# Shared weights for the last two latent tiles, four gathers inside the choice block, and a group norm inside it

## Chip, cores and metric

One core of a Trainium2 chip. The metric is the device time of one execution in microseconds, of which the median of several runs is given. Engines: PE (TensorE), DVE (VectorE), ACT (ScalarE), POOL (GpSimd), and SP, which only issues DMAs here. DMAs run on 16 DMA engines that all queues share.

## The reference

A two-layer backbone over 256 context tokens (two tiles of 128) and 512 latent tokens (four tiles), width 1024, all in float32. Each layer is a modulated norm, a mixer, and a product-key mixture of experts:

```python
def peer(h, wq, sub_keys, u_tab, v_tab):
    q = (h @ wq).reshape(T, P_HEADS, 2, P_DKEY // 2)            # 8 heads, two halves of 128
    s = jnp.einsum("thpd,hpnd->thpn", q, sub_keys)              # 16 x 128 key scores per token
    sv, si = lax.top_k(s, P_TOPK)                               # best 16 of each half
    cand = sv[:, :, 0, :, None] + sv[:, :, 1, None, :]          # 256 sums per head
    fv, fi = lax.top_k(cand, P_TOPK)                            # best 16: expert numbers
    gate = jax.nn.softmax(fv, axis=-1)
    a = gelu(u_tab[eidx] . h) * gate                            # 128 experts per token
    return sum(a * v_tab[eidx])
```

The mixer of layer 0 is a differential attention (4 heads, whose output gets a norm per head, `a_gn`, times 0.8) beside a windowed attention with sinks (8 heads); the two are joined and multiplied by `e_w_out`, gated and added to the stream. Layer 1 has a latent attention and a gated linear attention. Layer 1 needs only the latent tiles at the end.

## The kernel before

Everything for one token tile lies in 128 partitions. Raw blocks of five engine programs follow one another, each block ending in a barrier of all engines; within a block each engine works its own instruction list in order and waits on semaphores.

**Experts** (`run_experts`, L2652). For each tile there are 128 slots, one for each of a token's experts. In a slot POOL gathers 128 rows of 8 KB (u and v of one expert for each token, 1.05 MB) into one of 8 buffers `ring` (L2747), DVE multiplies the u half by the normed stream and sums it up (L2840), ACT makes gelu, weight and a diagonal matrix (L2859, L2861, L2865), and PE adds diagonal times v half to the tile's sum (L2876). POOL may gather slot s when PE is done with slot s - 8. Layer 0 has 6 tiles, 768 slots; layer 1 has 4, 512 slots. Before the first slot of tile t POOL waits for its expert numbers (`chosen`).

**Work beside the slots.** An order written out by hand puts other work at slots. In layer 0 (`BesideFirst`): the choice of the next tile's experts on DVE (`choose`, planned by `ChoicePlan`: for each quarter of the scores a load 2 slots after it is ready, first step at least 6 slots later, 8 slots a quarter; then 18 steps spread up to slot 119 of the tile); the attention of the four latent tiles (`HeadUnits`, 8 units a tile, begun at slots 9k for the first tile and 73 + 15k for the others); and for each latent tile (`LatentMixer`, L2063: POST 79, PITCH 120) group norm, output projection from `e_w_out_tiles` (8 loads of 512 KB), norm, and `LateScores` (L1910): 16 query and key products from `p_wqk` (16 loads of 576 KB), begun at slot 123 + 120x, one head every 4.4 slots. The four tiles load all of this separately. From slot 440 on `NextFront` projects the first half of layer 1. In layer 1 `LatentPair` does attention, projection and late scores of the last two tiles at once, a head every 4.0 slots from slot 145.

**Ahead of the experts** (`first_choice`, L1701): for two tiles projection with `w_o` (8 loads), gate, norm, transposes, 2 x 16 queries and scores with `w_q` in 4 buffers, and DVE's choice for the first tile, ending with the expert numbers (L1691) and the gates (L1697). Its last queries and scores are those of the second tile. Ahead of that in layer 0 stands a block of its own, `head_norm` ("gn0", L435), which does the group norm of the two context tiles: load the gains, ACT squares (L503), DVE sums (L521), ACT root (L508), DVE scales (L528, L531).

Of the kernel before, what the change touches and what calls it, by code (L numbers as in the profile page):

```python
# [14 lines left out]
P = 128  # L15
# [167 lines left out]
def start(nc, m, a):  # L183
# [3 lines left out]
    with Stage(nc, "mod") as s:  # L187
# [7 lines left out]
        with nc.Block() as block:  # L195
# [7 lines left out]
            def _(act):  # L203
# [4 lines left out]
                act.dma_start(m.sink[:, :], rows(a["b_sink"])).then_inc(v_loaded, 16)  # L208
                act.dma_start(m.band[:, :, :], a["band"].rearrange("s p k -> p s k")).then_inc(streams_loaded, 16)
                act.dma_start(m.R[:, 0:CT, :], a["ctx"].rearrange("b (t p) d -> p (b t) d", p=P)).then_inc(streams_loaded, 16)  # L210
                act.dma_start(m.R[:, CT:NT, :], a["x"].rearrange("b (t p) d -> p (b t) d", p=P)).then_inc(streams_loaded, 16)
                act.dma_start(m.ident[:, :], a["ident"]).then_inc(streams_loaded, 16)
                act.wait_ge(dots_ready, 1)
                act.activation(dots[:, :], dots[:, :], ACT.Exp).then_inc(lam_exp_done, 1)
                act.wait_ge(streams_loaded, 64)
# [8 lines left out]
            def _(dve):  # L224
# [10 lines left out]
                dve.wait_ge(v_loaded, 80)  # L235
# [3 lines left out]
                dve.tensor_scalar(m.neg_sink[:, :], m.sink[:, :], -1.0, None, ALU.mult)  # L239
                dve.drain()  # L240
# [192 lines left out]


def head_norm(nc, m, a, name, buf, tiles, segs, rope=None, factor=1.0, beside=None):  # L435

    turns = len(tiles) // 2  # L440
    extra = None
    S = sum(g * d for _, g, d, _ in segs)
    G = sum(g for _, g, _, _ in segs)
    with Stage(nc, name) as s:
        sq = s.sb("sq", [P, 2, S])
        ss = s.sb("ss", [P, 2, G])
        gains = s.sb("gains", [P, sum(d for _, _, d, _ in segs)])
        loaded = s.sem("loaded")
        squared, summed, rooted = s.sems("squared", 2), s.sems("summed", 2), s.sems("rooted", 2)
        if rope:  # L450
            r0, nr, tables = rope
            cos, sin = s.sb("cos", [P, NT, nr]), s.sb("sin", [P, NT, nr])
            near, far = s.sb("near", [P, 2, G, nr]), s.sb("far", [P, 2, G, nr])
            scaled, near_ready = s.sems("scaled", 2), s.sems("near_ready", 2)

        if beside:
            extra = beside(nc, m, a, s)

        def parts(i, q):

            at = g0 = gain0 = 0
            for c, g, d, _ in segs:
                yield (buf[:, i * 2 + q + (tiles[0] if tiles[0] and buf.shape[1] == NT else 0), c:c + g * d]
                       .rearrange("p (g d) -> p g d", d=d),
                       sq[:, q, at:at + g * d].rearrange("p (g d) -> p g d", d=d), ss[:, q, g0:g0 + g],
                       gains[:, gain0:gain0 + d], g, d, g0)
                at, g0, gain0 = at + g * d, g0 + g, gain0 + d

        def table(tab, i, q, g):
            return tab[:, ds(i * 2 + q + tiles[0], 1), :].broadcast_to([P, g, nr])  # L470

        def pairs(x, which):
            return x.rearrange("p g (f two) -> p g f two", two=2)[:, :, :, which]

        with nc.Block() as block:
            @block.sync
            def _(sp):
                at = 0
                for _, _, d, gain in segs:
                    sp.dma_start(gains[:, at:at + d], rows(gain)).then_inc(loaded, 16)  # L480
                    at += d
                if rope:
                    sp.dma_start(cos[:, :, :], a[tables + "_cos"].rearrange("(t p) d -> p t d", p=P)).then_inc(loaded, 16)
                    sp.dma_start(sin[:, :, :], a[tables + "_sin"].rearrange("(t p) d -> p t d", p=P)).then_inc(loaded, 16)

                if extra:
                    extra.sync(sp)

            if extra:
                @block.tensor  # L490
                def _(pe):
# [2536 lines left out]
```

## Time and profile before

| | |
|---|---|
| median of 3 runs | 4478.88 us (4476.03 to 4489.6) |
| profiled execution | 4486.69 us |
| its span, first to last instruction | 4485.4 us |
| PE busy | 3780.7 us, 84% |
| DVE busy | 2606.0 us, 58% |
| moved by DMA | 1577.55 MB, mean 352 GB/s |
| of it by gathers | 1342.36 MB |
| mean granted TensorE clock | 0.956 |

All rows that follow are of the one profiled execution, times counted from its first instruction. The experts of layer 0 take about 525 to 2660 us, those of layer 1 from 3109 us to the end. A view by windows gives, for each stretch, what each engine was busy and, at the end, the granted clock, the mean busy share of the 16 DMA engines (slightly over 1 when they are full) and the rate. In the timeline SPq and POOLq stand for a queue's issue of DMAs. The records of L2840 come in pairs, a product and the read of its sum.

### The profile page before, as it was taken

Reading aid. Unit: us, or ns where it says so; the run is one execution under the profiler, and the core shown is the slowest. Engines: PE = TensorE matmul, PEld = TensorE weight load, DVE = VectorE, ACT = ScalarE, POOL = GpSimd, SP = SyncE. Lnnn points to the kernel's source line nnn. Section 1 sums busy time; section 2 is a strip of 40 time slices with the busy share of each in tenths; the row PEclk is TensorE's granted clock in tenths of the full one; section 3 lists DMA queues with packets and bytes.
Section 4 is the critical chain, followed back from the end, with each engine's and each line's share of the span. In section 5 each row is a group of like instructions: output and inputs, shape, how many; then the busy total and the mean of one; then the engine's idle time right before and its main releaser. Section 6 shows DMA issues by size and latency. Waiting matters only on the chain. (4 is left out here: it accounts for less than half of the span.)

```text
span 4485.4 us, 45108 instructions
## 1 busy us (share of the span) xinstructions
PE 3780.7 (84%) x12934; PEld 1931.3 (43%) x12934; DVE 2606.0 (58%) x5668; ACT 1746.1 (39%) x5153; POOL 1703.8 (38%) x1350
## 2 busy tenths in 40 slices
PE   5987789898899898888889968687889997877777
PEld 2443644454454454444444433456444452322222
DVE  3524687666766856755654442346765558666544
ACT  1112255445444544433333331422664433333333
POOL 0100144444344433444444431001434434656675
PEclk9988999999999999999999988799999999999999
DMA  4254799999999999999999981027999999999998
GB/s 171 113 221 168 266 421 403 420 420 420 401 420 418 417 420 413 420 417 421 417 420 422 419 338 62 4 78 249 399 374 404 422 421 411 416 421 421 421 421 358
DMA packets 252894, 1577.55 MB, mean 352 GB/s; under 512 B 31715, under 2 KB 45955, under 8 KB 81510
## 3 DMA queue, kind: packets, MB, share of 16 engines
q0 software_dynamic: 185088, 1342.36, 72.5%
q1 hardware_dynamic: 65622, 228.83, 13.7%
q10 hardware_dynamic: 1936, 3.48, 0.2%
q8 instruction: 103, 1.69, 0.2%
q14 instruction: 145, 1.19, 0.1%
HBM read 1566.20 MB, written 8.36 MB: 351 GB/s over the span
## 5 line engine op out<-in xcount | busy, mean ns | idle before, releaser
L2876 PE MATMUL ps<-ex_ring,ex_diag 128*128 128x512 f32 x5120 | 2496.4, 621 | 481.4 <-ACT ex_diag L2865 450.5
L2747 POOL DMA_INDIRECT ex_ring<-in_p_uv,expert x1280 | 1648.6, 1288 | 2239.7 <-PE ps L2876 1523.9
L2840 DVE SCALAR_TENSOR_TENSOR ex_ring<-ex_ring,H 128x1024 f32<-128x1024 f32 x1280 | 1560.2, 1224 | 1198.3 <-DMA ex_ring<-in_p_uv,expert 1151.3
L2876 PEld LDWEIGHTS ps<-ex_ring,ex_diag 128*128 128x128 f32 x5120 | 926.3, 195 | 1705.4 <-ACT ex_diag L2865 879.6
L2859 ACT ACTIVATE ex_act_w<-ex_dots 128x1 f32<-128x1 f32 x1280 | 258.2, 202 | 1558.6 <-DVE ex_ring L2840 1552.4
L2865 ACT ACTIVATE ex_diag<-ident_sb,ex_weight 128x128 f32<-128x128 f32 x1280 | 513.9, 401 | 92.6 <-issue 3.6
L2861 ACT ACTIVATE ex_weight<-ex_act_w,gates 128x1 f32<-128x1 f32 x1280 | 377.0, 295 | 91.6 <-issue 4.5
L655 PE MATMUL ps<-win_w,hT 128*128 128x512 f32 (+1 forms) x480 | 191.9, 557 | 1.9 <-PEq L280 1.4
L2027 PEld LDWEIGHTS ps<-bs_hT,bs_w 128*128 128x128 f32 x1024 | 128.2, 197 | 34.6 <-issue 34.6
L655 PEld LDWEIGHTS ps<-win_w,hT 128*128 128x128 f32 x480 | 90.4, 191 | 106.0 <-issue 103.9
L2027 PE MATMUL ps<-bs_hT,bs_w 128*128 128x128 f32 x1024 | 127.7, 279 | 0.3 <-issue 0.3
L2840 DVE DVE_READ_ACCUMULATOR ex_ring<-ex_ring,H 128x1 f32 x1280 | 104.9, 82 | 0.0
L2859 ACT ACT_TABLE_LOAD x72 | 92.4, 1283 | 1.8 <-PEq L1737 0.5
L670 ACT ACTIVATE ph_sq<-ps 128x512 f32<-128x512 f32 (+1 forms) x24 | 12.4, 517 | 160.6 <-PE ps L655 160.6
L871 PEld LDWEIGHTS ps<-KV,bs_probsT 128*128 128x128 f32 x480 | 62.9, 192 | 24.0 <-issue 24.0
L1794 PE MATMUL ps<-hTc,fc_w_q 128*128 128x128 f32 x512 | 64.1, 279 | 9.6 <-DMA fc_w_q<-in_p_wqk 8.2
L1794 PE MATMUL ps<-hT,fc_w_q 128*128 128x128 f32 x512 | 64.4, 279 | 7.3 <-DMA fc_w_q<-in_p_wqk 5.9
L700 DVE TENSOR_REDUCE ph_ss<-ph_sq 128x8 f32<-128x512 f32 (+1 forms) x24 | 14.1, 586 | 97.0 <-ACT ph_sq L670 97.0
L2152 PEld LDWEIGHTS ps<-bs_w,bs_hT 128*128 128x128 f32 x512 | 62.3, 192 | 15.7 <-issue 15.7
L2027 PE MATMUL ps<-K,bs_w 128*128 128x256 f32 x256 | 65.7, 379 | 0.0
L1794 PEld LDWEIGHTS ps<-hTc,fc_w_q 128*128 128x128 f32 x512 | 59.6, 192 | 13.0 <-DMA fc_w_q<-in_p_wqk 11.5
L1794 PEld LDWEIGHTS ps<-hT,fc_w_q 128*128 128x128 f32 x512 | 59.5, 192 | 11.0 <-DMA fc_w_q<-in_p_wqk 9.3
(439 smaller groups left out, 3291.7 us busy)
## 6 DMA issues: line engine op xcount, KB each, us to landing
bs_w<-in_p_wqk SPq DMA_DIRECT2D x80, 576.0 KB
fc_w_q<-in_p_wqk SPq DMA_DIRECT2D x64, 576.0 KB, 4.9
ca_mod_w<-in_w_mod SPq DMA_DIRECT2D x24, 1024.0 KB, 6.8
ex_ring<-in_p_uv,expert POOLq DMA_INDIRECT x1280
win_mod_w<-in_w_mod SPq DMA_DIRECT2D x16, 1024.0 KB, 4.8
bs_w<-in_e_w_out_tiles SPq DMA_DIRECT2D x32, 512.0 KB
win_w<-in_e_w_in SPq DMA_DIRECT2D x9, 1024.0 KB, 11.2
mod_mod_w<-in_w_mod SPq DMA_DIRECT2D x8, 1024.0 KB, 15.0
```

Of the source, the lines that this page charges most:

```text
L655: mm = pe.matmul(m.ps[:, u % 4, 0:halves * 256], m.hT[:, k, t * P:(t + 1) * P], pre.w[:, n % 2, 0:halves, k, :], start=(k == 0), stop=(k = ...
L700: dve.tensor_reduce(ss[:, u % 2, 0:groups(u)], heads(sq[:, u % 2], u), AX.X, ALU.add).then_inc(summed, 1)
L871: mm = pe.matmul(self.O[:, cols], self.probsT[:, r % 2, x * P:(x + 1) * P], KV[:, self.blocks(n)[j], vals], start=(j == 0), stop=(j == las ...
L1794: mm = pe.matmul(m.ps[:, 4 + u % 2, 0:P], w_q[:, u % RING, k * P:(k + 1) * P], m.hT[:, k, cols(u // NH)], start=(k == 0), stop=(k == KC - 1))
L2027: mm = pe.matmul(m.ps[:, self.q_banks[u % nq], 0:cols], w[:, j * P:(j + 1) * P], self.turned_of(self.tiles_of(u), j), start=(j == 0), stop ...
L2152: mm = pe.matmul(m.ps[:, 7, c % 4 * P:(c % 4 + 1) * P], self.hT[:, k, :], w[:, k * P:(k + 1) * P], start=(k == 0), stop=(k == KC - 1), ski ...
L2747: pool.indirect_dma_start(ring[:, r, :], None, uv_rows, bass.IndirectOffsetOnAxis(ap=expert[:, t % 2, n:n + 1], axis=0),).then_inc(landed[ ...
L2840: dve.scalar_tensor_tensor(out=ring[:, r, 0:D], in0=ring[:, r, 0:D], scalar=1.0, in1=h_of(t + t0), op0=ALU.mult, op1=ALU.mult, accum_out=d ...
L2859: act.activation(act_w[:, b:b + 1], dots[:, t % 2, n:n + 1], ACT.Gelu)
L2861: act.activation(weight[:, b:b + 1], act_w[:, b:b + 1], ACT.Copy, scale=gates[:, t % 2, n:n + 1])
L2865: act.activation(diag[:, b, :], m.ident[:, :], ACT.Copy, scale=weight[:, b:b + 1]).then_inc(diag_ready, 1)
L2876: mm = pe.matmul(mix_banks(t)[:, half, :], diag[:, b, :], ring[:, r, D + half * BANK:D + (half + 1) * BANK], start=(n == 0), stop=(n == SL ...
```

## The change

- `LatentMixer` works on groups of tiles, here [0], [1] and [2, 3], instead of on four single tiles. The last two share the output projection and the late scores: each weight is loaded once and used for both. `POST` and `PITCH` are replaced by explicit slots 79, 202, 337; the shared late scores begin at slot 400 and end at 470. The attention units begin at 73 + 10k, not 73 + 15k, so that both tiles are done by slot 337. Scores go to two buffers in turn (`score_of`).
- `first_choice` gets a POOL program: when the projection is done and the numbers are written, it gathers slots 0 to 3. `run_experts` starts at slot 4. The ring is allocated around both, and `w_o` and `w_q` of `first_choice` lie in it (w_o in buffers 0 to 3).
- The block gn0 goes. Its work stands at the head of the ACT and DVE programs of `first_choice` in layer 0, with the gains loaded and scaled in the very first block. The gate product of the first tile goes ahead of the scale's. `iota` is loaded once, in the first block.
- Smaller: `rest` holds 4 heads instead of 16, `hot` lies in the scores, and `sc_read` is raised after the numbers.

Its core:

```diff
+EARLY = 4
+def gather(pool, m, a, slot, t):
+    r = slot % m.ring.shape[1]
+    pool.indirect_dma_start(m.ring[:, r, :], None, a["p_uv"],
+                            bass.IndirectOffsetOnAxis(ap=m.expert[:, t % 2, slot % SLOTS:slot % SLOTS + 1], axis=0),
+                            ).then_inc(m.landed[r], 16)
...
-        w_o, w_q = s.sb("w_o", [P, KC, D]), s.sb("w_q", [P, RING, (KC + 1) * P])
+        w_o = m.ring[:, 0:EARLY, :].rearrange("p r d -> p (r d)").rearrange("p (k d) -> p k d", d=D)
+        w_q = m.ring[:, EARLY:, :].rearrange("p r d -> p (r d)")[:, 0:RING * (KC + 1) * P].rearrange("p (r d) -> p r d", r=RING)
...
+            @block.gpsimd
+            def _(pool):
+                pool.wait_ge(out_done, 4)
+                pool.wait_ge(chosen, 1)
+                for slot in range(EARLY):
+                    gather(pool, m, a, slot, 0)
...
                 def turn(n):
+                    if grouped:
+                        pe.wait_ge(o_ready, n + 1)
...
+                if grouped:
+                    for n in range(2):
+                        act.activation(gsq[:, n, :], src_of(tiles[n])[:, 0:A_HEADS * A_DV], ACT.Square).then_inc(gn_squared, 1)
...
+                dve.wait_ge(gate_loaded, 16)
+                gated(0, 0, D, 2)
                 dve.wait_ge(vec_loaded, 16 * (4 if stream else 3))
...
-        begin = [9 * k for k in range(2 * A_HEADS)] + [73 + 15 * k for k in range((XT - 1) * 2 * A_HEADS)]
...
+            at, ahead = b + 4 + 6 * n, 4 // n
+            out_slots.append([at + (2 * ahead + 3) * (c // ahead) + 2 * (c % ahead) for c in range(KC)])
...
+            at = out_slots[-1][-1] + 4
...
+            late_begin.append(at + self.LOAD + 3 + 6 * n)
...
+        n = 2 * A_HEADS
+        begin = [9 * k for k in range(n)] + [73 + 10 * k for k in range(3 * n)]
+        self.mixer = LatentMixer(m, a, s, place, [[0], [1], [2, 3]], begin, [79, 202, 337], [4.4, 4.4, 4.4])
...
-                for slot in range(T * SLOTS):
-                    t, n, r = slot // SLOTS, slot % SLOTS, slot % RING
-                    if n == 0 and t:
+                for slot in range(EARLY, T * SLOTS):
+                    t, n = slot // SLOTS, slot % SLOTS
+                    if n == 0:
                         pool.wait_ge(chosen, t)
...
-                head_norm(nc, m, a, "gn0", m.Qc, CTILES, [(0, A_HEADS, A_DV, a["a_gn"])], factor=1.0 - LAM_INIT)
```

## Rows read from the trace of the kernel before

**Rows 1.** Page, section 2: GB/s in 40 slices of 112.1 us.

```profile
GB/s 171 113 221 168 266 421 403 420 420 420 401 420 418 417 420 413 420 417 421 417 420 422 419 338 62 4 78 249 399 374 404 422 421 411 416 421 421 421 421 358
```

**Rows 2.** Products at L2840, what ended DVE's idle time before them: us, times.

```profile
  DMA ex_ring<-in_p_uv,expert: 1151.3, 893
```

**Rows 3.** Windows: us, busy (x) PE, PEld, DVE, ACT, POOL, PEclk, DMA share, GB/s.

```profile
560.00:700.00 140.00, 123.95 (x378) 61.27 (x377) 115.66 (x315) 78.26 (x216) 61.80 (x54) 0.94 1.01 421
1200.00:1240.00 40.00, 34.91 (x129) 20.14 (x128) 23.39 (x43) 18.79 (x57) 13.63 (x13) 0.91 0.91 369
3240.00:3400.00 160.00, 144.26 (x478) 70.53 (x479) 108.92 (x232) 96.60 (x243) 63.66 (x57) 0.99 0.98 374
3560.00:3700.00 140.00, 133.72 (x431) 75.35 (x431) 70.33 (x171) 49.34 (x168) 50.03 (x48) 1.00 1.02 422
3780.00:3820.00 40.00, 28.62 (x58) 10.95 (x59) 36.82 (x58) 16.65 (x49) 18.21 (x14) 0.96 0.99 379
```

**Rows 4.** DMA issues of the whole run: count, KB each.

```profile
bs_w<-in_p_wqk SPq DMA_DIRECT2D x80, 576.0 KB
bs_w<-in_e_w_out_tiles SPq DMA_DIRECT2D x32, 512.0 KB
```

**Rows 5.** Timeline: start us, us, engine line op, [idle before], group norm to projection.

```profile
402.55 1.28 ACT L508 ACT_TABLE_LOAD   x1
403.02 0.33 SPq L480 DMA_DIRECT2D gn_gains<-in_a_gn  x1
407.59 0.69 DVE L528 TENSOR_TENSOR Qc<-Qc,gn_ss 128x512 f32<-128x512 f32 x1
410.97 3.65 PE L1762 MATMUL ps<-ident_sb,Qc 128*128 128x128 f32 x16 [16.37 <-PEq L475]
411.32 3.74 SPq L1741 DMA_DIRECT2D fc_w_o<-in_e_w_out  x8
414.81 28.23 PE L1775 MATMUL ps<-fc_w_o,hTc 128*128 128x512 f32 x64 [0.19 <-DMA fc_w_o<-in_e_w_out]
```

**Rows 6.** Timeline, handover to the experts of layer 0.

```profile
500.17 14.58 SPq L1735 DMA_DIRECT2D fc_w_q<-in_p_wqk  x7
515.85 0.23 DVE L1691 TENSOR_SCALAR expert<-fc_num 128x128 uint32<-128x128 f32 x1
525.33 1.02 POOL L2747 DMA_INDIRECT ex_ring<-in_p_uv,expert  x1 [126.52 <-issue]
```

**Rows 7.** Windows of both handovers, columns as in rows 3.

```profile
516.00:536.00 20.00, 7.10 (x51) 5.84 (x49) 0.79 (x5) 3.01 (x8) 7.61 (x8) 0.81 0.50 174
524.00:528.00 4.00, 1.57 (x8) 1.07 (x8) 0.00 (x0) 1.50 (x2) 2.06 (x3) 1.00 0.26 49
3101.00:3116.00 15.00, 7.02 (x55) 6.08 (x53) 0.67 (x3) 3.01 (x8) 5.07 (x6) 0.88 0.39 127
```

**Rows 8.** Timeline, handover to the experts of layer 1.

```profile
3100.75 0.23 DVE L1691 TENSOR_SCALAR expert<-fc_num 128x128 uint32<-128x128 f32 x1
3109.41 0.97 POOL L2747 DMA_INDIRECT ex_ring<-in_p_uv,expert  x1 [295.16 <-POOLq L1737]
```

**Rows 9.** Timeline of PE, layer 1: score products, four slots apart.

```profile
3560.24 0.61 PE L2014 MATMUL ps<-bs_w,bs_qT 128*128 128x128 f32 x4
3571.34 0.61 PE L2014 MATMUL ps<-bs_w,bs_qT 128*128 128x128 f32 x4
```

**Rows 10.** Timeline of DVE, layer 1: first and last step of a squeezed choice.

```profile
3754.89 2.28 DVE L2764 TENSOR_TENSOR R<-val 128x2048 f32<-128x2048 f32 x1
3809.43 0.29 DVE L2811 TENSOR_TENSOR gates<-ex_shift,ex_total 128x128 f32<-128x128 f32 x1
```

**Rows 11.** Lines of DVE in 560:720, 880:1080, 3240:3400: busy, mean ns, idle before.

```profile
L2840 DVE SCALAR_TENSOR_TENSOR ex_ring<-ex_ring,H 128x1024 f32<-128x1024 f32 x64 | 77.2, 1221 | 22.7 <-DMA ex_ring<-in_p_uv,expert 21.7
L2840 DVE SCALAR_TENSOR_TENSOR ex_ring<-ex_ring,H 128x1024 f32<-128x1024 f32 x70 | 85.3, 1223 | 70.9 <-DMA ex_ring<-in_p_uv,expert 70.4
L2560 DVE COPY bs_oT<-ps 64x128 f32<-64x128 f32 x10 | 2.9, 289 | 41.4 <-PE ps L2498 41.4
```

## What the change will do to the time

> **What bounds the kernel now.** I read the slices of the page first [rows 1]. From slice 5 to slice 22 (560 to 2640 us, the experts of layer 0) and again from slice 28 on (the experts of layer 1) the rate stands at 374 to 422 GB/s; PE is nearly as full (124 of the 140 us from 560) [rows 3], so both have to be held against every step. The engine that consumes the gathers says which of them binds: DVE's product at L2840 sat idle 1151 us for gathers to land [rows 2], and the 140 us from 560 ran at 421 GB/s and DMA share 1.01. So in these two stages the time is the bytes that move, divided by 421 GB/s, wherever the 8 buffers of the ring keep the queue full. Three kinds of stretch are exceptions. Dips inside the experts: 369 GB/s in the 40 us from 1200, 379 in the 40 us from 3780, 374 over 160 us from 3240 [rows 3]. Two handovers, where nothing is gathered although the experts are already numbered [rows 6, 7]. And the serial stages in front, where one group norm stands alone in a block [rows 5]. A slot, one gather of 1.05 MB, is 2.49 us of DMA.
>
> **Part 1, shared weights.** The latent group for tiles 4 and 5 loads once what two groups loaded: 8 output tiles of 512 KB, 16 query and key tiles of 576 KB [rows 4], and, once less, a gate row and a norm row spread over 128 x 1024 f32, 0.52 MB each by that shape. That is 4.19 + 9.44 + 1.05 = 14.68 MB, all of it in the bound stage. By 421 GB/s: **-34.9 us**. PE does the same columns as before, only bunched: per head 8 products of 256 columns and two scores. The same pairing exists in layer 1, one head every 4 slots. There PE's score records at 3560.24 and 3571.34 are 11.1 us apart for 4 slots, 2.78 us a slot [rows 9], and DMA held 422 GB/s at 1.02 for 140 us [rows 3]. In layer 0 a pair of heads comes every 4.4 slots, so PE has more room than there: no loss taken. For the shared output (8 pieces of two tiles in 24 slots, from slot 353) PE's load is about 1.7 + 8 x 3.6 / 24 = 2.9 us a slot and DMA's (1.05 + 8 x 0.52 / 24) / 0.421 = 2.9 us: a tie, for which I take **+1 us** (0 to 4).
>
> **Part 2, the choice of tile 4 is squeezed.** Its last quarter of scores is now ready at slot 470 instead of 433, since the pair starts at 400. By the plan (load 2 later, first step 6 later, 8 slots for a quarter) the other 18 steps of the choice get slots 486 to 502 instead of 449 to 502. Layer 1 shows this squeeze: there the scores of tile 4 come late too (slot 212), the 18 steps lie in slots 228 to 245, from the candidate sums at 3754.89 to the gates at 3809.43 + 0.29 = 3809.72, 54.8 us for 17 products and the choice, while DMA supplies 17 slots in 17 x 2.49 = 42.3 us [rows 10]. DVE falls 12.5 us behind; the ring absorbs most; the 40 us from 3780 ran at 379 instead of 422, that is 40 x 43 / 422 = 4.1 us lost [rows 3]. In layer 0 it is 16 slots: 34 us of choice + 16 x 1.23 = 53.6 us against 39.8, 1.3 us more behind, which the ring can't absorb any more: **+5.5 us** (3 to 14; no gain is possible, since the steps are the same ones).
>
> **Part 3, denser heads.** Units of attention of slots 73 to 313 come every 10 slots, not every 15, 8 of them in 80 slots. The first eight units already run at a pitch of 9: in 160 us from 560 DVE waited 21.7 us for DMA at that product and the rate was 421 [rows 3, 11]. With the late scores beside them there is room too: in the 200 us from 880 it waited 70.4 us for DMA [rows 11], and 2.3 more units at about 4.3 us of DVE take 10 of that. Only where the choice of tile 2, the norm and the heads meet (slots 240 to 255) is DVE full already, and 40 x (421 - 369) / 421 = 4.9 us are lost today [rows 3]. A third more heads there adds 0.13 us a slot over some 15 slots: **+2 us** (0 to 8).
>
> **Part 4, the group norm joins.** Today ACT squares and loads its table from 402.55, while DVE waits for the gains, which SP asks for at 403.02; the block ends, PE turns 16 pieces from 410.97 in 3.65 us and projects from 414.81, when the first of w_o has landed, asked for at 411.32 [rows 5]. After, SP asks for w_o where it asked for the gains (8.3 us earlier), and DVE reduces at once: root at 403.9 behind the table load (402.55 + 1.28), scale and gain of tile 0 to 406.1, of tile 1 to 407.8 (estimates from passes of 0.7 us over 512 columns, two a tile, and the small ones between), PE turns tile 1 from 408.0 to 409.9 and projects. **-4.9 us** (3 to 5.6): the wait for w_o becomes a wait for the norm. The rest of the stage follows, since out, h turn and 32 queries are one chain on PE and the rows of gate and scale come 8.3 us earlier with w_o; what is late next in it is DVE's choice, which starts from the fourth score. The new order of DVE (gate product ahead of the scale) is free: h of tile 0 is wanted only when PE has projected tile 1. The loads moved into the first block (iota, gain) are two small ones beside the streams there, in a block that waits for 8 MB of modulation weights: 0 (0 to +0.5).
>
> **Part 5, four gathers leave early.** In layer 0 the numbers are written at 515.85 + 0.23 = 516.1; the block ends with PE's last score and POOL issues in the next one, at 525.33 [rows 6]; its end is some 8 us behind the numbers. From 516 to 536 the DMA share is 0.50: 10.0 us of idle [rows 7]. After, POOL issues at 516.3; its first bytes come 1.6 us after issue, as today (share 0.26 in 524 to 528 is 1.0 us of work, from 527.0 [rows 7]). That leaves 1 us idle behind the last of w_q. The four cover 4 x 2.49 = 10 us. But the last w_q load, issued at 514.7 [rows 6], now shares the engines with gathers; it may take two to three times its 1.4 us, and PE's last scores and the block's end with it, so that gather 4 comes about 1 us after the four have run dry. 10.0 - 1 - 1: **-8.0 us** (4 to 9.4). Layer 1 the same: numbers at 3101.0, POOL at 3109.41 [rows 8], share 0.39 over the 15 us from 3101 [rows 7], 9.15 us idle, less 0.6 to the first bytes and 1 at the block's end: **-7.5 us** (4 to 8.7). POOL's queue holds nothing else in this block, so its new wait (for the projection that frees w_o's place, long done) delays nobody. DVE's later wait for iota and shift rows at the start goes too; it costs nothing today, as gathers lay in the queue all the while (PE's and DVE's late start at the first slots moves no byte).
>
> A rule of the Trainium skill bears on this. What the row shows is that the last w_q load is asked for 1.4 us before the numbers are ready, so the two meet [rows 6]. The page "DMA: Bandwidth & Descriptors", section "Queues, rings and completion order", says that each engine alternates between the queues that have work, packet by packet; by it no load is pushed back behind all four gathers, and the block's end slips by a transfer or two, not by 10 us. By strict order of arrival it would slip by nothing, and the part would give 1 us more. Which of the two holds no row of before shows.
>
> **The sum.** -34.9 + 1 + 5.5 + 2 - 4.9 - 8.0 - 7.5 = -46.8 us. The profiled execution took 4486.69 us: 4439.9. The median of the timed runs is 4478.88, 7.8 lower, and the same difference gives **4432 us**. Everything behind the experts of layer 0 (2700 to 3040) shifts as it stands, and so does the slow stretch from 3240, whose limit isn't bytes.
>
> **Rivals.** A, the ring can't absorb the crowding: DVE's lag of 14 us at tile 4, and the lags of tiles 2 and 4 in full, are passed on to DMA (nothing absorbed): 13.8 + 2 x 4.9 + 4 for the projection = 27 instead of 8.5, so 4451. Against it stand the 4.1 of 12.5 us in layer 1. B, the handovers give only half: the early gathers push back the last w_q loads and with them the block, and the next gather finds the engines dry for 4 us each time: 4440. C, the gain is larger, since the ring absorbs all of it and the dips of today go with the second group: -34.9 - 5.6 - 18 = -58.5, 4420. D, slower than before, by the stretch at 3240: there units every 5.5 slots bring the engines into lockstep, DVE waits 41.4 us of 160 for PE's value products [rows 11], and the rate is 374 instead of 421 [rows 3]. If a pitch of 10 with late weights beside it did the same for slots 73 to 313, 240 slots x 2.8 us x 0.125 = 84 us would be lost, against 46.8 + 2 of gain: 4514. It decides where a unit's chain no longer fits its pitch; at a pitch of 9 without weights DVE waits for none of it [rows 11], so the point lies below 9 unless the weights matter. E, the change doesn't do what it says: the pair runs PE-bound from 353 to 466 by 0.3 us a slot, 34 us, and takes back the weights: 4465.
>
> **How the numbers follow.** The forecast 0.58, A 0.13, B 0.10, C 0.11, D 0.04, E 0.04. With every term at its best the sum is -55.6 us (4423), with every term at its worst -19.9 us (4459). A, B and C lie within or 3 us outside, D and E are left out; C and the spread of the runs of before put the low end at 4415, the worst sum the high end at 4460. A measurement of this kernel can tell about 0.3% (13 us) from no change. Faster by more than that: all but D and E (E is 12.8 us faster, within it), less 0.02 for the spread of medians, 0.90; within it 0.05; slower 0.05.
>
> **What would show it.** Right: bs_w loads of 24 and 64 instead of 32 and 80; POOL's first gather within 1 us of the numbers in both layers, DMA share above 0.9 over the following 20 us; PE's first projection at 410; the experts of layer 0 some 26 us shorter from first gather's landing to last; a dip of 5 us near slot 495. Wrong: the rate below 415 over slots 73 to 313 (D), below 400 over 353 to 466 (E), or a DMA gap after the fourth gather (B).

## The result, and the profile after

The changed kernel took **4408.23 us** (median of 4 runs, 4406.40 to 4418.11) against 4480.22 us for the kernel before (median of 4, 4476.03 to 4489.60): ratio 0.9843, 95% interval 0.9824 to 0.9861. It is 72.0 us faster where 46.8 were predicted, and 4408 lies below the low end of 4415. The profiled executions took 4407.58 and 4486.69 us, their spans 4406.3 and 4485.4.

The page of the changed kernel, section 2 (40 slices of 110.2 us), its DMA issues, and its windows at the places of rows 3:

```profile
GB/s 174 108 212 198 288 424 401 412 419 424 404 425 426 426 420 426 427 391 427 427 427 427 427 295 37 4 86 297 394 372 412 425 423 405 427 427 427 427 427 363
...
bs_w<-in_p_wqk SPq DMA_DIRECT2D x64, 576.0 KB, 8.0
bs_w<-in_e_w_out_tiles SPq DMA_DIRECT2D x24, 512.0 KB, 8.0
```

```profile
560.00:700.00 140.00, 125.92 (x387) 62.66 (x385) 114.98 (x307) 80.38 (x223) 59.44 (x54) 0.93 1.01 420
3780.00:3820.00 40.00, 31.36 (x65) 10.79 (x65) 30.14 (x97) 14.39 (x48) 26.25 (x17) 1.00 1.01 428
```

The loads are 24 and 64 in place of 32 and 80 [rows 4], and the bytes fell from 1577.55 to 1562.74 MB. The surprise is in the slices. Before, no slice stood above 422 GB/s [rows 1]; after, half of the busy slices read 426 or 427, in the experts of layer 1 too, where the change has nothing to do with the weights. **The ceiling itself rose by 1.2%.** The prediction divided every byte by 421 GB/s and held that number for fixed.

The group norm, then the handover to the experts of layer 0 (timelines of the changed kernel, columns as in rows 5):

```profile
394.34 1.15 ACT L1747 ACTIVATE fc_gsq<-Qc 128x512 f32<-128x512 f32 x2 [8.14 <-PEq L867]
395.50 1.28 ACT L1750 ACT_TABLE_LOAD   x1
396.03 3.73 SPq L1634 DMA_DIRECT2D ring<-in_e_w_out  x8
398.90 3.42 PE L1663 MATMUL ps<-ident_sb,Qc 128*128 128x128 f32 x16 [11.31 <-DVE Qc L1797]
402.15 1.02 PE L1676 MATMUL ps<-ring,hTc 128*128 128x512 f32 x2
...
503.77 0.23 DVE L1570 TENSOR_SCALAR expert<-fc_num 128x128 uint32<-128x128 f32 x1
504.89 1.02 POOL L1586 DMA_INDIRECT ring<-in_p_uv,expert  x1 [113.09 <-DVE expert L1570]
507.90 1.01 PE L1705 MATMUL ps<-ring,fc_qT 128*128 128x128 f32 x4
508.72 0.94 POOL L1586 DMA_INDIRECT ring<-in_p_uv,expert  x1 [0.30 <-issue]
519.23 1.23 DVE L2787 SCALAR_TENSOR_TENSOR ring<-ring,H 128x1024 f32<-128x1024 f32 x1 [14.02 <-PEq L1630]
519.93 1.34 POOL L1586 DMA_INDIRECT ring<-in_p_uv,expert  x1 [10.28 <-POOLq L1630]
```

POOL issues its first gather 0.9 us behind the numbers, as meant. But gather 4 follows only at 519.93: from 509.7 to 519.2 no engine computes. Nothing but the four gathers is in flight, and the next block begins when they have landed: in the DMA records of the trace their last packet ends at 518.4, 0.8 us before DVE starts. The windows of that handover (columns as in rows 3) show the engines of the DMA full, then empty again:

```profile
504.00:508.00 4.00, 4.00 (x38) 4.00 (x37) 0.71 (x3) 0.98 (x4) 2.50 (x3) 1.00 0.44 114
508.00:512.00 4.00, 0.78 (x5) 0.40 (x3) 0.00 (x0) 0.75 (x3) 1.35 (x2) 0.89 0.98 395
512.00:516.00 4.00, 0.00 (x0) 0.00 (x0) 0.00 (x0) 0.00 (x0) 0.00 (x0) 0.50 1.01 422
516.00:520.00 4.00, 0.77 (x3) 0.74 (x5) 0.77 (x1) 0.81 (x1) 0.07 (x1) 0.50 0.36 152
520.00:524.00 4.00, 4.00 (x10) 1.87 (x8) 4.00 (x7) 3.17 (x10) 3.39 (x3) 0.50 0.51 143
```

**Where the time went.** I cut the profiled span of each kernel at two marks, the instruction that writes the expert numbers in layer 0 and the one in layer 1. The first mark moves by chance: the last value product of the context attention began at 393.50 before and 386.48 after, and anywhere from 386.48 to 408.05 in the 14 profiles of this study, among them profiles of kernels that don't differ before it. The latest of them had a granted clock of 0.56 from 350 to 386, where before had 0.94 and after 1.00. So the front is compared from that product on, and the rest from mark to mark.

| us | before | after | |
|---|---|---|---|
| start to the attention's last value product | 393.5 | 386.5 | -7.0, chance |
| from there to the numbers of layer 0 | 122.3 | 117.3 | -5.0 |
| numbers of layer 0 to those of layer 1 | 2584.9 | 2531.4 | -53.5 |
| numbers of layer 1 to the end | 1384.6 | 1371.1 | -13.5 |

The last row alone contradicts the prediction, which had 7.5 us there, all of it from early gathers.

### The profile page after: what moved, and what is told of

It is laid out like the page before. It is cut to its first block and busy times, and to the rows that moved or that the text cites. A ratio compares the mean times of both kernels' runs of the same rounds, so it can differ in the third digit from the quotient of the medians.

```text
span 4406.3 us, 44443 instructions
## 1 busy us (share of the span) xinstructions
PE 3757.3 (85%) x12678; PEld 1911.6 (43%) x12678; DVE 2603.1 (59%) x5667; ACT 1746.1 (40%) x5137; POOL 1689.1 (38%) x1350
## 2 busy tenths in 40 slices
DMA packets 248572, 1562.74 MB, mean 355 GB/s; under 512 B 30851, under 2 KB 44963, under 8 KB 77190
## 5 line engine op out<-in xcount | busy, mean ns | idle before, releaser
L2823 PE MATMUL ps<-ring,ex_diag 128*128 128x512 f32 x5120 | 2476.7, 618 | 416.6 <-ACT ex_diag L2812 389.7
L1586 POOL DMA_INDIRECT ring<-in_p_uv,expert x1280 | 1633.8, 1276 | 2179.3 <-PE ps L2823 1447.4
L2787 DVE SCALAR_TENSOR_TENSOR ring<-ring,H 128x1024 f32<-128x1024 f32 x1280 | 1557.5, 1225 | 1084.0 <-DMA ring<-in_p_uv,expert 1041.2
L2823 PEld LDWEIGHTS ps<-ring,ex_diag 128*128 128x128 f32 x5120 | 923.9, 194 | 1663.6 <-ACT ex_diag L2812 847.5
L1945 PEld LDWEIGHTS ps<-hTc,bs_w 128*128 128x128 f32 x768 | 110.8, 191 | 29.3 <-issue 23.5
L1945 PE MATMUL ps<-hTc,bs_w 128*128 128x128 f32 (+1 forms) x768 | 120.3, 310 | 0.3 <-issue 0.3
L2787 DVE DVE_READ_ACCUMULATOR ring<-ring,H 128x1 f32 x1280 | 105.2, 82 | 0.0
L1695 PE MATMUL ps<-hTc,ring 128*128 128x128 f32 x512 | 65.0, 282 | 8.0 <-DMA ring<-in_p_wqk 6.8
L1695 PE MATMUL ps<-hT,ring 128*128 128x128 f32 x512 | 63.9, 278 | 7.7 <-DMA ring<-in_p_wqk 6.2
L2090 PEld LDWEIGHTS ps<-bs_w,hTc 128*128 128x128 f32 x512 | 60.9, 192 | 11.5 <-issue 11.5
```

The costliest lines, as they stand in the source:

```text
L1586: pool.indirect_dma_start(m.ring[:, r, :], None, a["p_uv"], bass.IndirectOffsetOnAxis(ap=m.expert[:, t % 2, slot % SLOTS:slot % SLOTS + 1] ...
L1695: mm = pe.matmul(m.ps[:, 4 + u % 2, 0:P], w_q[:, u % RING, k * P:(k + 1) * P], m.hT[:, k, cols(u // NH)], start=(k == 0), stop=(k == KC - 1))
L1945: mm = pe.matmul(m.ps[:, self.q_banks[u % nq], 0:cols], w[:, j * P:(j + 1) * P], self.turned_of(self.tiles_of(u), j), start=(j == 0), stop ...
L2090: mm = pe.matmul(m.ps[:, 7, at:at + P], self.hT[:, k, i * P:(i + 1) * P], w[:, k * P:(k + 1) * P], start=(k == 0), stop=(k == KC - 1), ski ...
L2787: dve.scalar_tensor_tensor(out=ring[:, r, 0:D], in0=ring[:, r, 0:D], scalar=1.0, in1=h_of(t + t0), op0=ALU.mult, op1=ALU.mult, accum_out=d ...
L2823: mm = pe.matmul(mix_banks(t)[:, half, :], diag[:, b, :], ring[:, r, D + half * BANK:D + (half + 1) * BANK], start=(n == 0), stop=(n == SL ...
```

## The experiments

### Is the rate the ring's address?

The buffers of the ring are where the gathered rows land. Adding up the allocations, `ex0_ring` starts at byte 99264 of a partition in the kernel before and `ex1_ring` at 101312; both are 192 past a multiple of 256 (the residue, as it is called below). The change adds two lasting tiles, `iota` (64 bytes a partition) and `gain_gn` (512), and allocates the ring elsewhere: 108032 and 110080, both multiples of 256. Theory: that residue sets the rate. Rivals: the chip or the run; another part of the change.

```diff
# x1_before_pad64: the kernel before, and this line
+        m.pad = ctx.enter_context(nc.sbuf_tensor("pad", [P, 16], F32))
# x2_after_pad448 (112 floats), x5_after_pad256 (64), x6_after_pad64 (16): the changed kernel, in both layers
-                with nc.sbuf_tensor("ring1", [P, 8, 2 * D], F32) as m.ring:
+                with nc.sbuf_tensor("pad1", [P, 112], F32), nc.sbuf_tensor("ring1", [P, 8, 2 * D], F32) as m.ring:
```

> The kernel before with one unused tile of 64 bytes a partition among its lasting allocations, so that the ring of expert rows starts at byte 99328 of a partition (a multiple of 512) in place of 99264 (448 past one); in layer 1 at 101376 in place of 101312. Nothing else differs. Address theory (the start address of the ring sets how fast the rows land): the stretch 560:700 moves 427 GB/s in place of 421, and as the expert stages are mostly saturated the time falls by 30 to 50 us, to about 4440. Rival (the rate differed by chip or by run, or comes from another part of the change): 421 GB/s and 4480 within 5.

> The changed kernel with an unused tile of 448 bytes a partition just ahead of each layer's ring, so that both rings start 448 bytes past a multiple of 512, as in the kernel before. Address theory: 421 GB/s again in saturated stretches and 30 to 50 us more than the changed kernel, about 4448. Rival (rate by chip, run or another part of the change): 427 GB/s and 4408 within 5.

> The changed kernel with 256 unused bytes a partition ahead of each ring: rings start at a multiple of 256 that is no multiple of 512. Where the grain of the address is 256 bytes: 427 GB/s in saturated stretches, 4408 within 5. Where it is 512 bytes or more: 421 GB/s and 30 to 40 us more, about 4441.

> The changed kernel with 64 unused bytes ahead of each ring: rings start 64 bytes past a multiple of 512. Grain of 256 or 512 bytes: 421 GB/s and about 4441, as with 448. Grain of 64 bytes, with something else at work in the earlier two pads: 427 GB/s and 4408.

The GB/s of the page, section 2, of the four in this order:

```profile
GB/s 173 107 213 188 265 427 406 426 426 426 409 425 426 417 425 420 426 426 427 425 426 427 427 333 55 4 79 261 399 374 405 425 423 418 421 426 427 426 427 366
```

```profile
GB/s 173 114 219 184 291 419 402 403 419 421 409 421 421 416 419 422 422 390 421 422 422 422 422 292 40 4 94 296 394 368 414 420 421 402 422 421 421 421 421 356
```

```profile
GB/s 174 107 213 190 287 427 400 419 417 423 404 425 425 421 423 426 427 392 427 427 427 427 427 303 38 4 92 291 396 369 413 425 423 406 427 427 427 427 427 364
```

```profile
GB/s 173 114 217 184 290 419 403 411 416 420 406 416 420 412 415 420 421 386 421 421 422 422 421 295 43 4 93 295 393 370 406 421 420 402 421 421 421 421 421 356
```

| kernel | ring start mod 256 | highest GB/s | us, median | layer 0 to layer 1 | layer 1 to end |
|---|---|---|---|---|---|
| before | 192 | 422 | 4480.22 | 2584.9 | 1384.6 |
| x1_before_pad64 | 0 | 427 | 4434.86 | 2550.4 | 1371.5 |
| after | 0 | 427 | 4408.23 | 2531.4 | 1371.1 |
| x5_after_pad256 | 0 | 427 | 4407.63 | 2526.3 | 1373.1 |
| x2_after_pad448 | 192 | 422 | 4441.40 | 2550.0 | 1385.3 |
| x6_after_pad64 | 64 | 422 | 4448.24 | 2553.8 | 1387.3 |

Every expectation of the address theory was met. One unused tile of 64 bytes makes the old kernel 48.9 us faster than the runs of before beside it (4483.73; ratio 0.9887, 0.9860 to 0.9914); moving the new kernel's ring off the multiple costs it 33.2 and 40.0 us. The pad of 256 puts the ring at an odd multiple of 256 and costs nothing, so **a multiple of 256 is enough, it needn't be one of 512**, and 64 past is about as bad as 192 past. No ring was placed 128 past, so the grain may be 128 bytes as well as 256. The pads shift the tiles behind them as well. Of these `bs_w`, the other large target, can be left out as cause: in layer 0 it starts at residue 0 in x2, at 422, and at 128 in x1, at 427. DVE's product on the ring took the same in all six, a median of 1.22 us, so it isn't the engines' reading of the ring. Chip and run are out too, as x1 and x2 ran on one chip in one job.

The single packets say the same. A row of 8 KB is one packet, 163,840 of them in a run. With the ring at residue 0, 98% took 309 ns or less (all eleven profiles); in before, x2 and x6 it was 24 to 27%, and 71 to 74% took 311 to 320 ns. It isn't a matter of gathers alone: of the 6272 packets of 8 KB that plain loads moved between 40 and 400 us, 1183 took 311 to 320 ns in before, where their targets lie 192 past, and 41 to 90 in the thirteen others, where they lie at 0. On 128 past there is a hint only: the first block's 8 loads of modulation weights land 64 past in before and 128 past in the others, and of their 1024 packets 342 took 311 to 320 ns in before, 30 to 254 in the others.

The Trainium skill, page "DMA: Bandwidth & Descriptors", section "How a descriptor splits into AXI transactions", says that a descriptor is cut into transactions of 256 bytes, and that one which doesn't start 256-byte aligned needs one more. By it a row of 8 KB takes 33 in place of 32, 3.1% more (an estimate). The runs agree on the sign, and with its 256 bytes as far as they were tried; the measured difference is 1.2% (422 against 427 GB/s). The page speaks of what a transaction can read; that it is the landing address that counts here is what the pads show. Why the loss is a good third of what this count gives, and the same 64 and 192 past, no run shows.

### Do the early gathers buy anything?

The prediction's Part 5 said 15.5 us. The timeline above suggested another account, that the block's end waits until the gathers have landed.

```diff
# x3_early0: N = 0, and run_experts' POOL doesn't wait for `chosen` at slot 0.  x11_early2: N = 2
-                for slot in range(EARLY):
+                for slot in range(N):
                     gather(pool, m, a, slot, 0)
...
-                for slot in range(EARLY, T * SLOTS):
+                for slot in range(N, T * SLOTS):
```

> The changed kernel with no early gathers: the first choice issues none, the expert stage issues all from slot 0. Drain theory (the end of the block waits until the early gathers have landed, so they buy only the few us between the numbers and that end): 3 us more in each layer, 4414 in all (4408 to 4418). The prediction's own term (8.0 and 7.5 us gained): 15.5 us more, about 4424.

> The changed kernel with two early gathers in place of four. Drain theory (the block's end waits for the last early gather to land): the first gather of the expert stage is issued about 5 us sooner after the numbers (11 us in place of 16.2), and the time from layer 0's numbers to layer 1's stays within 1 us of the changed kernel's 2531.4 us; 4408. The prediction's term (2 us gained by each early gather, both layers): 4416.

From x3_early0's timeline, then from x11_early2's:

```profile
525.33 0.23 DVE L1570 TENSOR_SCALAR expert<-fc_num 128x128 uint32<-128x128 f32 x1
531.85 1.05 PE L1705 MATMUL ps<-ring,fc_qT 128*128 128x128 f32 x4
534.31 1.02 POOL L1586 DMA_INDIRECT ring<-in_p_uv,expert  x1 [120.94 <-issue]
539.86 1.23 DVE L2787 SCALAR_TENSOR_TENSOR ring<-ring,H 128x1024 f32<-128x1024 f32 x1 [13.12 <-DMA ring<-in_p_uv,expert]
```

```profile
508.37 0.23 DVE L1570 TENSOR_SCALAR expert<-fc_num 128x128 uint32<-128x128 f32 x1
510.81 0.97 POOL L1586 DMA_INDIRECT ring<-in_p_uv,expert  x1 [0.30 <-issue]
517.02 1.01 PE L1705 MATMUL ps<-ring,fc_qT 128*128 128x128 f32 x4
521.06 1.35 POOL L1586 DMA_INDIRECT ring<-in_p_uv,expert  x1 [9.28 <-POOLq L1630]
```

Without early gathers the next block's first gather goes out 1.4 us behind PE's last score product (532.90 to 534.31); with four it is 11.0 us (508.91 to 519.93). And the first product of the experts comes 14.5 us behind the numbers with none (539.86 - 525.33), 15.5 us with four (519.23 - 503.77): the early gathers delayed the very stage that they were to feed. From the numbers of layer 0 to the end of the span it is 3902.7 us with none, 3902.8 with two, 3902.5 with four. **They buy nothing that can be seen**; the same kernel with a pad of 256 differs by more (3899.4). The medians of whole runs (4418.43, 4410.58 and 4408.23) don't contradict it: those of x3_early0 lie between 4406.25 and 4441.22, with two at the level of the changed kernel and two late. Of these the profiled one (4429.27) is late by the chance in the front that the table above sets aside; the other has no profile.

The drain theory was right on the wait and missed on its price and its details. It gave each layer 3 us for the early gathers, and they bought none. With two of them the block restarted 12.7 us behind the numbers, not 11, and layer 0 to layer 1 took 2534.9 us, not within 1 us of 2531.4 (the rest of the run was 3.2 us shorter; no run shows why). The 12.7 us come from the gathers' own landing: the last load of w_q was asked for at 508.9, 0.6 us ahead of the first gather, the two shared the engines, and the second gather's last packet ended at 519.6. Layer 1 of the same run shows the wait with PE long done:

```profile
3048.08 1.01 PE L1705 MATMUL ps<-ring,fc_qT 128*128 128x128 f32 x4
3053.65 1.23 DVE L2787 SCALAR_TENSOR_TENSOR ring<-ring,H 128x1024 f32<-128x1024 f32 x1 [9.33 <-PEq L1630]
3054.34 1.35 POOL L1586 DMA_INDIRECT ring<-in_p_uv,expert  x1 [7.85 <-POOLq L1630]
```

In the four handovers with early gathers (layers 0 and 1 of the changed kernel, then of x11_early2) the last packet of the last gather ended at 518.4, 3050.0, 519.6 and 3053.0, and the next block's first product on DVE began at 519.2, 3050.8, 520.4 and 3053.7, 0.7 to 0.8 us behind each. So it is shown that the gathers in flight hold the block.

### Sharing, and denser heads

```diff
# x4_single and x7_single_dense: the latent tiles 2 and 3 apart again (and W = 2, so that nothing else changes size)
-        self.mixer = LatentMixer(m, a, s, place, [[0], [1], [2, 3]], begin, [79, 202, 337], [4.4, 4.4, 4.4])
+        self.mixer = LatentMixer(m, a, s, place, [[0], [1], [2], [3]], begin, [79, 199, 319, 439], [4.4, 4.4, 4.4, 4.4])
# x4_single also: heads 15 slots apart, as before
-        begin = [9 * k for k in range(n)] + [73 + 10 * k for k in range(3 * n)]
+        begin = [9 * k for k in range(n)] + [73 + 15 * k for k in range(3 * n)]
# x8_pace36: the changed kernel, late scores of the pair 3.6 slots apart
-[79, 202, 337], [4.4, 4.4, 4.4])
+[79, 202, 337], [4.4, 4.4, 3.6])
# x9_pitch12_pace36, on top of x8; then x9b_pitch15_9, on top of x8, with 346 for 337
+        begin = [9 * k for k in range(n)] + [73 + 12 * k for k in range(n)] + [169 + 10 * k for k in range(2 * n)]
+        begin = [9 * k for k in range(n)] + [73 + 15 * k for k in range(n)] + [193 + 9 * k for k in range(2 * n)]
```

> The changed kernel with the latent tiles 2 and 3 apart again (groups of one tile, begun every 120 slots) and the heads 15 slots apart as before; group norm, early gathers and the ring's address stay. The prediction's terms (34.4 us for 14.68 MB at 427 GB/s, less 5.5 for the squeezed choice, 2 for denser heads, 1 for the wide outputs): 26 us more than the changed kernel, about 4434. Rival (the ring absorbs the squeezed choice and the heads): 34 us more, 4442. Rival (dips cost twice the terms): 18 us more, 4426.

> The changed kernel with the latent tiles 2 and 3 apart (as x4_single), but with the heads 10 slots apart as in the change: the density of the heads by itself, against x4_single. The prediction's term: 2 us more than x4_single (0 to 8), about 4433. Reading of the rates in 60 us stretches of both traces (the changed kernel loses 11 us more than x4_single before slot 190, where only the heads' pitch differs): 11 us more than x4_single, about 4442. Ring absorbs it: 4431 and the same rates as x4_single.

> The changed kernel with the late scores of the shared group 3.6 slots apart in place of 4.4, so that the scores of tile 4 are there about 12 slots earlier and its choice has some 38 slots in place of some 26. The squeezed choice costs what the prediction says (5.5 us, rates of 383 and 406 GB/s between 1847 and 1967): 2 to 5 us less than the changed kernel, about 4404. Rival (the dip is that of the group's late scores themselves, denser still): same or up to 5 us more.

> x8_pace36 with the heads of latent tile 1 begun 12 slots apart (73 to 157) in place of 10, those of the shared pair 10 apart from slot 169. Theory (dense heads cost 11 to 16 us by dips before slot 190): tile 1's half of it comes back, 3 to 6 us less than x8_pace36, about 4397. Rival (only the number of heads before some slot counts, the loss moves with them into the pair's part): 4402, the dips later in the stage.

> x8_pace36 with the heads of tile 1 begun 15 slots apart as in the kernel before, those of the shared pair 9 apart from slot 193, and the pair's norm begun at slot 346 in place of 337. Theory of dense heads: tile 1's part like x4_single (a gain of 6 to 8 us before slot 190), the pair's part 1 slot denser (a loss of 2 to 4 us): 4398. Rival (9 apart is past what the engines keep up with): over 4405.

To see where bytes are lost I cut layer 0's experts into 31 windows of 60 us from 24 us behind the numbers on, and added up 60 us x (ceiling - rate) / ceiling (ceiling 427, for before 422):

| kernel | heads' pitch | windows 1-13 | 14-21 | 22-31 | layer 0 to layer 1 | us, median |
|---|---|---|---|---|---|---|
| before | 15 | 13.6 | 5.3 | 4.1 | 2584.9 | 4480.22 |
| x1_before_pad64 | 15 | 11.4 | 5.2 | 1.3 | 2550.4 | 4434.86 |
| x4_single | 15 | 9.1 | 6.9 | 3.0 | 2550.2 | 4430.75 |
| x7_single_dense | 10 | 26.1 | 3.7 | 4.2 | 2567.8 | 4446.80 |
| after | 10, shared | 20.2 | 2.8 | 9.4 | 2531.4 | 4408.23 |
| x8_pace36 | 10, shared | 21.4 | 3.5 | 3.7 | 2528.6 | 4401.65 |
| x9_pitch12_pace36 | 12/10, shared | 22.2 | 2.2 | 4.1 | 2526.7 | 4408.04 |
| x9b_pitch15_9 | 15/9, shared | 25.6 | 3.4 | 6.2 | 2532.1 | 4411.75 |

**Denser heads cost 16.1 us with the tiles apart** (x7 against x4: 4446.80 - 4430.75; 17.6 mark to mark), where the prediction had 2 and at most 8. **From x7 to the changed kernel 38.6 us are gained** (36.4 mark to mark), against the 34.4 us of the shared bytes at 427 GB/s. That step isn't sharing alone. The second group also begins at slot 202 in place of 199, and 5.9 us of the step lie in windows 1 to 13 (26.1 against 20.2), which end at slot 285, before anything is shared. The five other profiles with the changed kernel's order up to there (x3, x5, x8, x10, x11) lose 19.4 to 22.3 us in them, so it is no chance; that the three slots do it is likely, but no run moves them alone. From window 14 on x7 loses 7.9 us and the changed kernel 12.2, so that sharing with its squeezed choice is worth 34.4 - 4.3 = **about 30 us**, and denser heads cost **about 11** in the change as it is (20.2 - 9.1). Both together gain 22.5 us (x4 to after; 18.8 mark to mark), where the terms for x4_single gave 26.

Windows of x4_single, x7_single_dense and x9_pitch12_pace36, the sixth, the eleventh and the twelfth of the 31 (columns as in rows 3):

```profile
829.60:889.60 60.00, 54.59 (x193) 28.51 (x192) 38.23 (x62) 29.16 (x87) 29.23 (x23) 0.97 1.01 426
1129.60:1189.60 60.00, 48.45 (x154) 24.47 (x153) 54.32 (x89) 34.66 (x83) 26.14 (x20) 0.94 1.01 426
1189.60:1249.60 60.00, 57.33 (x239) 33.59 (x238) 31.81 (x52) 29.43 (x94) 25.55 (x23) 1.00 1.01 415
```

```profile
829.80:889.80 60.00, 51.68 (x193) 28.44 (x193) 37.99 (x68) 31.00 (x90) 21.83 (x20) 0.91 0.98 392
1129.80:1189.80 60.00, 53.06 (x215) 30.77 (x215) 51.68 (x102) 32.79 (x85) 22.76 (x20) 0.94 0.96 373
1189.80:1249.80 60.00, 54.76 (x209) 30.67 (x208) 42.81 (x75) 35.70 (x96) 25.35 (x22) 0.97 1.01 415
```

```profile
832.30:892.30 60.00, 57.38 (x216) 31.96 (x217) 37.82 (x63) 29.07 (x91) 23.58 (x22) 0.95 1.01 426
1132.30:1192.30 60.00, 53.81 (x222) 31.34 (x221) 53.35 (x97) 33.88 (x89) 26.26 (x20) 0.94 0.97 393
1192.30:1252.30 60.00, 52.80 (x201) 30.46 (x200) 31.18 (x58) 30.17 (x86) 20.55 (x20) 0.91 0.95 370
```

In the eleventh window DVE already works 54 of 60 us with heads 15 apart (a choice lies there), at 426 GB/s; with heads 10 apart PE rises from 48 to 53 of 60 beside it and the rate falls to 373. The changed kernel, also 10 apart, holds 416 there with both engines busier still (PE 56, DVE 55), so the busy shares alone don't account for the loss. Twelve apart clears the sixth window (426) and moves the loss into the eleventh and twelfth (393 and 370). My theory for x9 fell, its rival stood: the loss goes with the units to where they meet the choice. Nor did 15 and 9 do better. Neither is shown to beat x8_pace36: x9 is 1.9 us shorter from mark to mark, 6.4 us longer by the medians, and the two come from different jobs, whose runs of before differ by 4.7. Which of PE and DVE is late in those windows the runs don't settle.

The squeezed choice is the other dip. The first two rows are of the changed kernel, the last two of x8_pace36:

```profile
1847.80:1907.80 60.00, 42.02 (x79) 14.96 (x77) 56.83 (x132) 19.84 (x60) 26.46 (x20) 0.91 0.95 383
1907.80:1967.80 60.00, 50.31 (x114) 21.04 (x114) 42.95 (x96) 28.30 (x87) 31.84 (x26) 0.94 1.00 406
```

```profile
1850.90:1910.90 60.00, 48.26 (x111) 19.34 (x112) 56.19 (x112) 26.62 (x81) 30.74 (x26) 1.00 1.00 415
1910.90:1970.90 60.00, 47.38 (x102) 18.53 (x100) 38.63 (x87) 25.88 (x77) 34.84 (x25) 0.94 1.01 425
```

DVE is busy 56.8 of 60 us with the choice of tile 4 and PE only 42.0: here it is DVE that starves the ring. The two windows lose 9.1 us, and giving the choice some 12 more slots leaves 2.0 of it. x8_pace36 is the fastest kernel of the study: 4401.65 us (4399.15 to 4408.25), ratio to before 0.9807 (0.9779 to 0.9834), 6.0 us under x5_after_pad256 of the same job. Its interval overlaps that of the changed kernel (0.9824 to 0.9861), so that it is faster than the change is likely, not shown; the vanished dip is shown.

### The group norm

x10_gn_apart is the changed kernel with the block gn0 back.

```diff
                 context_attention(nc, m, a)
+                head_norm(nc, m, a, "gn0", m.Qc, CTILES, [(0, A_HEADS, A_DV, a["a_gn"])], factor=1.0 - LAM_INIT)
...
-                first_choice(nc, m, a, 0, CTILES, 1, a["e_w_out"], 0, lambda t: m.Qc[:, t, :], lambda t: m.H[:, t, :], True)
+                first_choice(nc, m, a, 0, CTILES, 1, a["e_w_out"], 0, lambda t: m.Qc[:, t, :], lambda t: m.H[:, t, :])
```

> The changed kernel with the group norm of layer 0 in a block of its own again, ahead of the first choice. The prediction's term: 4.9 us more (3 to 5.6), 4413. Reading of both traces from the first square to the projection (7.3 us against 13.4): 6.1 us more, 4414, and the projection starts 13.4 us after the first square.

```profile
400.57 1.15 ACT L506 ACTIVATE gn_sq<-Qc 128x512 f32<-128x512 f32 x2 [8.20 <-PEq L993]
402.21 0.33 SPq L483 DMA_DIRECT2D gn_gains<-in_a_gn  x1
405.05 0.23 DVE L518 TENSOR_SCALAR gn_gains<-gn_gains 128x128 f32<-128x128 f32 x1 [8.43 <-DMA gn_gains<-in_a_gn]
410.18 3.36 PE L1789 MATMUL ps<-ident_sb,Qc 128*128 128x128 f32 x16 [16.42 <-PEq L478]
414.24 6.08 PE L1802 MATMUL ps<-ring,hTc 128*128 128x512 f32 x13 [0.70 <-DMA ring<-in_e_w_out]
```

From the first square to the projection it is 13.7 us apart (400.57 to 414.24) and 7.8 us joined (394.34 to 402.15): 5.9 us. From the attention's last value product to the numbers, apart 122.3, 122.8 and 123.4 us (before, x1, x10), joined 114.3 to 117.3 in eleven profiles, mean 116: about **7 us**. The median of whole runs, 4421.07 (4413.59 to 4443.24), is 12.8 above the changed kernel's; it holds the chance of the front as well and is too wide to size a term of 5. By the ratios to the runs of before beside them (0.9858 and 0.9843) it is about 7, with intervals as wide as that.

## Why the prediction was right or wrong

**Direction right, size wrong, and the missing size has one cause.** The step that failed is "the time is the bytes that move, divided by 421 GB/s". That number was read rightly [rows 3] and taken for fixed, while it hung on where this kernel's ring lay: the changed kernel moved its bytes at 427. Like with like, the change from the kernel before to x2_after_pad448, which has the old residue, is -42.3 us (4483.73 to 4441.40), and to x6_after_pad64 -34.6 (4482.86 to 4448.24), against -46.8 predicted. The rest, 33 to 40 us, is the ring's address, which no term, rival or bound held: every term at its best gave 4423, rival C 4420, and all of them were worked out at 421 GB/s. The diff shows what moved it: the ring's new place and two lasting tiles ahead of it.

- **Part 1, -34.9 and +1.** Held: 24 and 64 loads, 14.81 MB less in all; the 14.68 MB reckoned are 34.4 us at 427 GB/s. The tie feared in the shared output didn't show; from 1308 to 1788 the eight windows of the changed kernel stand at 415 to 426 GB/s. E is refuted. The account closes: 34.4 us of bytes and 34.0 - 32.4 = 1.6 us less lost in the windows give 36.0, against 36.4 measured mark to mark from x7 to the changed kernel. Together with Part 2 it was -28.4, against some -30.
- **Part 2, +5.5 (3 to 14).** Held: windows 22 to 31 lose 9.4 us against 3.0 in x4_single and 3.7 in x8_pace36, so 5.7 to 6.4. The reading from layer 1 [rows 10] carried.
- **Part 3, +2 (0 to 8).** Mis-sized: 11.1 in windows 1 to 13 of the change itself (20.2 - 9.1), and 16.1 with the tiles apart. The step that failed is "with the late scores beside them there is room too". It joined two stretches [rows 11]: 560 to 720, where heads come 9 apart beside a choice but no projection, late score or norm runs, and 880 to 1080, where late scores run but heads come 15 apart. The prediction looked at the one place where all of them meet, slots 240 to 255, but x7 loses 60 x (426 - 373) / 427 = 7.4 us more than x4 in the one window from 1130, slots 219 to 238, just ahead of it, where that window holds a choice, a norm and 64 products of the output projection (7.8 us of PE) beside the heads. D had the mechanism at five to eight times its price.
- **Part 4, -4.9 (3 to 5.6).** The square-to-projection distance shrank by 5.9 us, the whole front by about 7. The wait for w_o became a wait for the norm, as meant: PE's turning waited 11.3 us for DVE, and the estimates of DVE's passes were a little slow.
- **Part 5, -15.5.** Wrong, the whole term: 0. The step that failed is "gather 4 comes about 1 us after the four have run dry". It treated the end of the block as PE's last score. In fact the block doesn't end with gathers in flight, so that the engines idle 9.5 us and DMA has a hole from about 517.4 to 522 in place of the one before the first gather (shares of 0.36 and 0.51 of two windows of 4 us, the busy part at the front of the first and at the end of the second). B named the hole and priced it at half; it took all. The share above 0.9 for 20 us, named as the sign, was there for 8 to 9 us. The meeting of the last w_q load with the gathers, for which the prediction took 1 us, didn't come about in layer 0: the load had landed at 505.4, the gathers' first packet started at 506.6, and PE's last score product ended 5.1 us behind the numbers, before 8.1. In x11_early2 they did meet, and the load's last packet ended 5.7 us behind its issue, against 6.1 before and 6.0 in x3_early0 with no gather beside it. The rule of the Trainium skill quoted in the prediction ("DMA: Bandwidth & Descriptors", "Queues, rings and completion order") has each engine alternate between its queues, packet by packet, so that no load is pushed back behind gathers, and the trace of x11_early2 agrees.
- **The sum.** With the ring at residue 0: denser heads +11, sharing with the squeezed choice in it -30, group norm -7, early gathers 0, together -26; measured from x1_before_pad64 to the changed kernel -26.6 (4434.86 to 4408.23). At the old residues the same edits gain 34.6 and 42.3, so 8 to 16 us more. A slower supply leaves the engines more slack and hides more of their crowding; with this it fits that the loss in the 31 windows grew by 14.5 us at residue 0 (x1 to the change), but by 4.3 and 9.0 at the old ones (before to x2 and x6). No run took it apart.

Errors ran both ways. Parts 3 and 5 were 9 + 15.5 = 24.5 us too good, Parts 1 and 2 some 2 and Part 4 2.1 us too poor, and the address then brought 33 to 49. A hit at 4432 would have been luck.

## What to carry to other kernels

When a kernel is bound by DMA, work out the start address of the tiles that the bulk of the bytes lands in before you cost anything: a start 64 or 192 bytes past a multiple of 256 cost 1.2% of the rate here, and any edit that allocates, moves or resizes a tile ahead of it changes the result by that, for better or worse, apart from what it is meant to do. Where a rate enters every term, ask what it rests on before it is called a ceiling. An unused tile of a few bytes is both the cure and the control experiment. And work issued early into a block buys time only if the block's end doesn't wait for it.

## What the runs showed of the hardware

- Gathers of 8 KB rows into SBUF ran at 427 GB/s where the ring started at a multiple of 256 bytes (eleven kernels) and at 422 where it started 64 or 192 bytes past one (three). Over the 1280 gathers of 1.05 MB this is 33 to 49 us. A packet of 8 KB took 309 ns at most in 98% of cases there, and 311 to 320 ns in 71 to 74% here. 256 past a multiple of 512 was as good as 0; 128 past wasn't tried for the ring.
- Four gathers in flight held the end of a block open: 9.5 us with all engines idle (509.7 to 519.2). In four handovers the next block began 0.7 to 0.8 us behind the last gather's last packet; with none in flight its first gather was issued 1.4 us behind PE's last product.
- The start of the kernel varies by itself: the context attention's last value product began anywhere from 386.5 to 408.1 us in 14 profiles. In the latest the granted clock from 350 to 386 was 0.56, most of the stretch at the lower of the two levels (1.2 and 2.4 GHz), where before, after, x1 and x8 had 0.94 to 1.00.
